# Moving the p_2 load behind the first expert tiles, and its transposes ahead of the gathered rows' transposes, in a two-block transformer kernel

## The chip, the cores and the metric

The kernel runs on one core of a Trainium2 chip. The metric is the device time of one execution in microseconds (us). Three runs of the kernel before took 2132.51, 2132.94 and 2133.28 us, median 2132.94. Everything is float32.

The engines are TensorE (PE, with its weight loads as PEld), VectorE (DVE), ScalarE (ACT), GpSimd (POOL) and SyncE (SP). SP does no arithmetic here; it waits on semaphores and issues nearly all DMA transfers.

## The reference

The input is one sequence of 256 tokens with 1024 features. A first block runs two layers, each a gated delta rule branch and a differential attention branch. A second block runs one layer: a pooling and dilated attention mixer, then a mixture of experts, then a gated projection of a second input `p` (256 tokens x 256 features), and a last norm. The change touches the passage from the mixer into the experts:

```python
x = x + jnp.einsum('bse,ed->bsd', mix, w_out[i])
x = x + moe(rmsnorm_2(x, g_ffn[i]), w_router[i], b_router[i], w_gate_up[i],
            b_gate_up[i], w_down[i], b_down[i])
gate = jax.nn.sigmoid(jnp.einsum('bsd,de->bse', rmsnorm_2(x, g_ple[i]), w_ple_gate[i]))
x = x + jnp.einsum('bsp,pd->bsd', p[i], w_ple_proj[i]) * gate
```

`moe` sends each token to its best 4 of 32 experts. An expert has a gate and up matrix of 1024 x 2048 and a down matrix of 1024 x 1024:

```python
gu = xb @ w_gate_up[e] + b_gate_up[e]
g, u = gu[:, :D_EXPERT], gu[:, D_EXPERT:]
g = jnp.minimum(g, SWIGLU_LIMIT)
u = jnp.clip(u, -SWIGLU_LIMIT, SWIGLU_LIMIT)
glu = g * jax.nn.sigmoid(SWIGLU_ALPHA * g)
return ((u + 1.0) * glu) @ w_down[e] + b_down[e]
```

## The kernel before

Each engine has its own program, written out by hand in order; there is no scheduler. An engine goes on in its order until a wait on a semaphore that another engine or a DMA raises. A transfer raises its semaphore by 16 when it has landed.

**The experts.** All 32 experts are computed for whatever tokens chose them, up to 64 tokens in one round. An expert's weights are six tiles of 2 MB: four of `w_gate_up_2` (j = 0 to 3) and two of `w_down_2` (j = 4, 5). The tiles T = 0, 1, 2, ... go round eight buffers of 2 MB in the order of `SEQ`; five of them are in the SBUF tensor `ring`, three in `region`. PE raises `tile_used` once for each tile that it is through with, and before the first expert by eight at once (L996). SP loads T0 to T3 while the mixer runs and T4 to T7 when the mixer has ended (`x_mixed` at 4), since their buffers hold mixer data until then. From T8 on SP waits for `tile_used` at T + 1, that is until PE is through with tile T - 8: T8 waits for T0, and T12 for T4, the first down tile of expert 0.

**SP around the change.** After `x_mixed`, SP issues in this order: `ptok` (the tokens of `p_2`, 256 KB, semaphore `ple_in`), the down biases (128 KB), the two gate and up biases (128 KB each) and `one_of` (80 KB) on `bias_in`, then T4 to T7, then the waiting loads from T8 on. All have line L402, that of the helper `load`. A row that names `p_dram` is the load of `ptok`.

**PE before the first expert.** The router's ranks end in one-hot matrices `P1` (DVE, L2100). `gather()` (L1006) multiplies them with `h2` and so picks the rows of expert 0 into bank 3. ACT copies them into `Xs` (L1487, semaphore `X_sb`), `turn_gathered()` transposes them on PE (L1013, `XT_ps`), and ACT copies the result into `XT` (L1491, `XT_sb`). Expert 0 begins when `XT_sb` is there: its bias products (L1054), then its gate and up products (L1062), the gather for expert 1, `down_biases()` (L1035), transposes (L1074, L1078, L1013) and the down products (L1088).

**The transposes of ptok** (L1100, four of 128 x 128 into bank 2, after a wait for `ple_in` at 16) stand between `turn_gathered()` and expert 0. ACT copies them into `pT` at L1497 (`pT_sb`), after its copy into `XT`. `pT` is used by `down_biases()` only as a wait (bank 2 must be free), and as data after the last expert.

Of the kernel before, what the change touches and what calls it, by code (L numbers as in the profile page):

```python
# [13 lines left out]
P = 128  # L14
# [105 lines left out]
def block_kernel(nc, a, out):  # L120
    ctx = ExitStack()
    with ctx:
# [5 lines left out]
        def s(name):  # L128

            if name not in sems:  # L130
                sems[name] = ctx.enter_context(nc.semaphore(name))
            return sems[name]
# [8 lines left out]
        def once(signal):  # L141
            return next(s(name) for name, signals in ONCE.items() if signal in signals)
# [89 lines left out]
        def view(at, n):  # L232
            return region[:, at:at + n]
# [16 lines left out]
        def units(ap):  # L250
            return ap.rearrange("p (u c) -> p u c", c=P)
# [43 lines left out]
        T, V = units(T_f), units(V_f)  # L295
# [26 lines left out]
        ptok = view(2048, 512).rearrange("p (t c) -> p t c", t=NT)  # L322
# [77 lines left out]
        def _(sp):  # L400
            def load(dst, src, name, **kw):
                sp.dma_start(dst, src, **kw).then_inc(s(name), 16)  # L402
# [56 lines left out]
            for n in range(4):  # L459
                c = (n + 1) % 4 * NB  # L460
# [20 lines left out]
            def expert_tile(T, e):  # L481

                j, slot = T % 6, SEQ[T % 8]
                if j < 4:
                    src = gate_up_src[ds(e * D + j * 256, 256), :].rearrange("(p k) n -> p (k n)", k=2)
                else:
                    src = down_src[ds(e * D + (j - 4) * 512, 512), :].rearrange("(p k) n -> p (k n)", k=4)
                load(slot_mem(slot), src, f"w_in_slot{slot}")
# [6 lines left out]
            load(brow, a["b_router_2"].broadcast_to([P, NE]), "ffn_in")  # L495
            load(grow, a["g_ffn_2"].broadcast_to([P, D]), "g_ffn_in")
            sp.wait_ge(s("x_mixed"), 4)
            load(ptok, a["p_2"][0, 0].rearrange("(t p) c -> p t c", p=P), "ple_in")
            load(biases[0:NE, :], a["b_down_2"][0], "bias_in")
            for g in range(2):  # L500
                load(biases[NE * (g + 1):NE * (g + 2), :], a["b_gate_up_2"][0, :, g * D:(g + 1) * D], "bias_in")
            load(one_of, a["c_one_of"], "bias_in")
            for T in range(4, 8):
                expert_tile(T, T // 6)
            for T in range(8, 6 * GROUP):
                sp.wait_ge(s("tile_used"), T + 1)
                expert_tile(T, T // 6)
# [16 lines left out]
            for u in range(4):  # L524
                t, g = divmod(u, 2)
# [6 lines left out]
        def _(pe):  # L532
# [38 lines left out]
            for l in range(DEPTH):  # L571
# [14 lines left out]
                for u in range(12):  # L586
# [4 lines left out]
                    for b in range(2):  # L591
                        c = (2 * (u % 2) + b) * P
# [50 lines left out]
                for u in range(12):  # L643
                    t = u % 2
# [199 lines left out]
                for u in range(4):  # L844
                    t, g = divmod(u, 2)
# [164 lines left out]
            def turn_gathered():  # L1010

                for c in range(4):
                    mm = pe.transpose(pb[3][:, c * P:(c + 1) * P], Xs4[:, c // 2, c % 2, :], ident)  # L1013
                mm.then_inc(s("XT_ps"), 1)
# [77 lines left out]
            pe.wait_ge(s("onehot"), 1)  # L1092
            pe.wait_ge(s("h2_sb"), NT)
            gather()
            pe.wait_ge(s("X_sb"), 1)
            turn_gathered()
            pe.wait_ge(s("ple_in"), 16)
            for t in range(NT):
                for k in range(2):
                    mm = pe.transpose(pb[2][:, k * S + t * P:k * S + (t + 1) * P], ptok[:, t, k * P:(k + 1) * P], ident)  # L1100
            mm.then_inc(once("pT_ps"), 1)
            for q in range(GROUP):
                expert(0, q)
            rounds = pe.value_load(rounds_i[0:1, 0:1], min_val=1, max_val=ROUNDS)
# [36 lines left out]
        def _(act):  # L1141
# [347 lines left out]
            def turned(n):  # L1489
                act.wait_ge(s("XT_ps"), n)  # L1490
                act.activation(XT, pb[3][:, :].rearrange("p (c h t) -> p c h t", c=4, h=2), ACT.Copy).then_inc(s("XT_sb"), 1)  # L1491

            act.preload_act_table_set("sigmoid_and_others")
            gathered(1)
            turned(1)
            await_once(act, "pT_ps")
            act.activation(pT, pb[2][:, :].rearrange("p (k t) -> p k t", k=2), ACT.Copy).then_inc(once("pT_sb"), 1)  # L1497

            def sigmoids(i):
                act.wait_ge(s("g_clamped"), i + 1)  # L1500
                act.activation(sg, gm, ACT.Sigmoid, scale=1.702).then_inc(s("sig"), 1)  # L1501
# [724 lines left out]
```

## Time and profile before

| | |
|---|---|
| median of 3 runs | 2132.94 us (2132.51 to 2133.28) |
| the profiled execution's own time | 2132.51 us |
| its span, first to last instruction | 2130.7 us |
| PE busy | 2040.8 us, 96% |
| DVE, ACT, POOL busy | 739.3, 445.9, 106.7 us |
| moved by DMA | 551.27 MB, mean 259 GB/s |
| mean granted TensorE clock | 0.990 of full speed |

The time is 1.8 us more than the span, and what lies outside the span is not touched here. Busy shares alone do not say what bounds the kernel: PE is busy for 96% of the span, in the expert stage too, yet a chain of waits can still pass through a transfer. The sections of the profile to read together are the rate of the DMA over the span, the chain that ended last, and the order of SP's transfers with the time at which each landed.

### The profile page before, as it was taken

Reading aid. Unit: us, or ns where it says so; the run is one execution under the profiler, and the core shown is the slowest. Engines: PE = TensorE matmul, PEld = TensorE weight load, DVE = VectorE, ACT = ScalarE, POOL = GpSimd, SP = SyncE. Lnnn points to the kernel's source line nnn. Section 1 sums busy time; section 2 is a strip of 40 time slices with the busy share of each in tenths; the row PEclk is TensorE's granted clock in tenths of the full one; section 3 lists DMA queues with packets and bytes.
Section 4 is the critical chain, followed back from the end, with each engine's and each line's share of the span. In section 5 each row is a group of like instructions: output and inputs, shape, how many; then the busy total and the mean of one; then the engine's idle time right before and its main releaser. Section 6 shows DMA issues by size and latency. Waiting matters only on the chain.

```text
span 2130.7 us, 23346 instructions
## 1 busy us (share of the span) xinstructions
PE 2040.8 (96%) x9042; PEld 1043.9 (49%) x9042; DVE 739.3 (35%) x2021; ACT 445.9 (21%) x1073; POOL 106.7 (5%) x84
## 2 busy tenths in 40 slices
PE   7999999999999999999998999999999999999998
PEld 6754777544875577644454333333333333333334
DVE  4559566211567665511143111111111111111112
ACT  2151454311124245311131000000000000000003
POOL 0022121000013112000000000000000000000000
PEclk9999999999999999999998999999999999999999
DMA  6643211342453312236634999999999999999993
GB/s 215 238 152 125 80 41 40 119 158 95 158 223 119 119 41 80 80 118 247 231 127 180 401 428 428 428 428 428 428 428 428 428 428 429 428 428 428 428 426 116
DMA packets 103066, 551.27 MB, mean 259 GB/s; under 512 B 9005, under 2 KB 13521, under 8 KB 77906
## 3 DMA queue, kind: packets, MB, share of 16 engines
q1 hardware_dynamic: 101138, 549.73, 64.1%
q8 instruction: 47, 0.77, 0.1%
q10 hardware_dynamic: 1856, 0.56, 0.1%
q14 instruction: 25, 0.20, 0.0%
HBM read 547.07 MB, written 3.21 MB: 258 GB/s over the span
## 4 chain that ended last, share of the span: by engine, by line
PE 77%; DMA 17%; DVE 4%; ACT 1%; issue 1%; SPq 0%; DVEq 0%; ACTq 0%
PE bank L557 26%; PE bank L1062 13%; DMA ring<-w_gate_up_dram 8%; DMA region<-w_gate_up_dram 8%; PE bank L1088 7%; PE bank L807 5%; PE bank L669 3%; PE bank L860 3%; PE bank L1020 2%; PE bank L1006 2%; PE bank L681 2%; PE bank L944 1%; PE bank L692 1%; PE bank L1054 1%; DVE region L1873 1%
## 5 line engine op out<-in xcount | busy, mean ns | idle before, releaser
L1062 PE MATMUL bank<-ring,region 128*64 128x512 f32 x1280 | 286.3, 596 | 16.2 <-DMA ring<-w_gate_up_dram 16.2
L2135 DVE TENSOR_SCALAR region<-bank 128x512 f32<-128x512 f32 x32 | 22.1, 692 | 718.1 <-PE bank L1062 718.1
L557 PE MATMUL bank<-ring,hT 128*128 128x512 f32 (+1 forms) x464 | 194.8, 577 | 0.0
L1062 PEld LDWEIGHTS bank<-ring,region 128*64 128x64 f32 x1280 | 87.6, 137 | 212.1 <-issue 174.3
L1062 PE MATMUL bank<-region 128*64 128x512 f32 x768 | 172.2, 595 | 13.5 <-DMA region<-w_gate_up_dram 13.5
L557 PE MATMUL bank<-ring,region 128*128 128x512 f32 x400 | 175.3, 598 | 4.5 <-ACT region L1154 4.5
L557 PE MATMUL bank<-hT,ring 128*128 128x256 f32 x768 | 173.8, 389 | 3.4 <-DMA ring<-w_in_dram 3.4
L557 PEld LDWEIGHTS bank<-hT,ring 128*128 128x128 f32 x768 | 149.2, 195 | 27.2 <-issue 6.0
L1088 PE MATMUL bank<-ring,region 128*64 128x512 f32 x640 | 142.6, 595 | 10.5 <-DVE region L2145 6.9
L557 PEld LDWEIGHTS bank<-ring,hT 128*128 128x128 f32 x464 | 87.5, 190 | 99.9 <-issue 98.5
L1501 ACT ACTIVATE region<-region 128x512 f32<-128x512 f32 x32 | 20.2, 630 | 519.8 <-DVE region L2135 519.8
L557 PEld LDWEIGHTS bank<-ring,region 128*128 128x128 f32 x400 | 76.0, 191 | 100.3 <-issue 95.0
L669 PE MATMUL bank<-ring,hT 128*128 128x512 f32 x256 | 123.2, 593 | 0.0
L1062 PEld LDWEIGHTS bank<-region 128*64 128x64 f32 x768 | 53.1, 137 | 129.8 <-issue 103.0
L807 PE MATMUL bank<-ring,hT 128*128 128x512 f32 x256 | 111.5, 592 | 0.0
L1088 PEld LDWEIGHTS bank<-ring,region 128*64 128x64 f32 x640 | 47.4, 137 | 89.2 <-issue 89.2
L1088 PE MATMUL bank<-region 128*64 128x512 f32 x384 | 86.2, 597 | 3.5 <-DVE region L2145 3.5
L2201 POOL TENSOR_TENSOR region<-ring,c_main_sb 128x512 f32<-128x512 f32 x48 | 64.4, 1346 | 281.9 <-PE bank L681 281.9
L1668 DVE SCALAR_TENSOR_TENSOR region<-region,conv_wT 128x256 f32<-128x256 f32 x192 | 78.0, 477 | 0.0
L807 PEld LDWEIGHTS bank<-ring,hT 128*128 128x128 f32 x256 | 48.0, 190 | 57.4 <-issue 57.4
L1505 ACT ACTIVATE region<-bank 128x512 f32<-128x512 f32 x32 | 19.1, 597 | 222.2 <-PE bank L1088 222.2
L1006 PE MATMUL bank<-region 128*64 128x512 f32 x264 | 63.7, 604 | 0.2 <-DVE region L2100 0.2
(343 smaller groups left out, 2350.3 us busy)
## 6 DMA issues: line engine op xcount, KB each, us to landing
ring<-w_gate_up_dram SPq DMA_DIRECT2D x80, 2048.0 KB, 31.0
region<-w_gate_up_dram SPq DMA_DIRECT2D x48, 2048.0 KB, 32.2
ring<-w_in_dram SPq DMA_DIRECT2D x44, 2048.0 KB, 7.9
ring<-w_down_dram SPq DMA_DIRECT2D x40, 2048.0 KB, 35.3
region<-w_down_dram SPq DMA_DIRECT2D x24, 2048.0 KB, 35.3
ring<-w_out_dram SPq DMA_DIRECT2D x5, 2048.0 KB, 7.9
ring<-rows_scratch SPq DMA_DIRECT2D x4, 2048.0 KB, 9.7
ring<-w_pa_dram SPq DMA_DIRECT2D x4, 2048.0 KB, 7.7
```

Source lines behind the costliest of these rows:

```text
L557: mm = pe.matmul(dst, lhs(k), w(k), start=(k == 0), stop=(k == n_k - 1))
L669: mm = pe.matmul(pb[3][:, :], hT[:, k, t * P:(t + 1) * P], w[:, k, :], start=(k == 0), stop=(k == KC - 1))
L681: mm = pe.matmul(pb[V_BANK[q]][:, u * P:(u + 1) * P], Lv[q][:, u, :], T[:, u, :], start=True, stop=True)
L807: mm = pe.matmul(pb[GATE_BANKS[kind][t]][:, :], hT[:, k, t * P:(t + 1) * P], w[:, k, :], start=(k == 0), stop=(k == KC - 1))
L860: mm = pe.matmul(pb[i % 4][:, :], hT[:, k, t * P:(t + 1) * P], slot_w(slot)[:, k, :], start=(k == 0), stop=(k == KC - 1))
L1006: mm = pe.matmul(pb[3][hf * 64:(hf + 1) * 64, :], P1[:, t, :], h2[:, t, hf * NB:(hf + 1) * NB], start=(t == 0), stop=(t == 1))
L1020: mm = pe.matmul(pb[4 + 2 * t + hf][:, :], CT[hf * 64:(hf + 1) * 64, t, :], ysb[hf * 64:(hf + 1) * 64, :], start=False, stop=False, skip_g ...
L1062: mm = pe.matmul(pb[g][hf * 64:(hf + 1) * 64, :], XT[:, 2 * (j % 2) + kk, j // 2, :], wj[:, kk, c:c + NB], start=False, stop=(j == 3 and k ...
L1088: mm = pe.matmul(pb[2][hf * 64:(hf + 1) * 64, :], actT[:, c, j, :], wj[:, c, hf * NB:(hf + 1) * NB], start=(j == 0 and c == 0), stop=(j == ...
L1668: ins = dve.scalar_tensor_tensor(dst, src, w, dst, ALU.mult, ALU.add)
L2135: dve.tensor_scalar(gm, pb[0][:, :], 7.0, None, ALU.min).then_inc(s("g_clamped"), 1)
L2201: pool.tensor_tensor(Lv[q].rearrange("p (d t) c -> p d t c", d=2), LT_all[:, n].rearrange("p (d t) c -> p d t c", d=2), lvl[:, q].unsqueez ...
```

## The change

It has three parts. On SP, T4 is issued first after `x_mixed`, then the biases and `one_of`, then T5 to T7, and `ptok` last, ahead of the first load that waits for `tile_used`. On PE, the wait for `ple_in` and the four transposes of `ptok` stand ahead of the wait for `X_sb` and `turn_gathered()`. On ACT, the copy into `pT` stands ahead of the copy into `XT`. Nothing is added or removed. Lines behind L498 move by one.

```diff
--- before.py
+++ after.py
@@ -495,13 +495,14 @@
             load(brow, a["b_router_2"].broadcast_to([P, NE]), "ffn_in")
             load(grow, a["g_ffn_2"].broadcast_to([P, D]), "g_ffn_in")
             sp.wait_ge(s("x_mixed"), 4)
-            load(ptok, a["p_2"][0, 0].rearrange("(t p) c -> p t c", p=P), "ple_in")
+            expert_tile(4, 0)
             load(biases[0:NE, :], a["b_down_2"][0], "bias_in")
             for g in range(2):
                 load(biases[NE * (g + 1):NE * (g + 2), :], a["b_gate_up_2"][0, :, g * D:(g + 1) * D], "bias_in")
             load(one_of, a["c_one_of"], "bias_in")
-            for T in range(4, 8):
+            for T in range(5, 8):
                 expert_tile(T, T // 6)
+            load(ptok, a["p_2"][0, 0].rearrange("(t p) c -> p t c", p=P), "ple_in")
             for T in range(8, 6 * GROUP):
                 sp.wait_ge(s("tile_used"), T + 1)
                 expert_tile(T, T // 6)
@@ -1092,13 +1093,13 @@
             pe.wait_ge(s("onehot"), 1)
             pe.wait_ge(s("h2_sb"), NT)
             gather()
-            pe.wait_ge(s("X_sb"), 1)
-            turn_gathered()
             pe.wait_ge(s("ple_in"), 16)
             for t in range(NT):
                 for k in range(2):
                     mm = pe.transpose(pb[2][:, k * S + t * P:k * S + (t + 1) * P], ptok[:, t, k * P:(k + 1) * P], ident)
             mm.then_inc(once("pT_ps"), 1)
+            pe.wait_ge(s("X_sb"), 1)
+            turn_gathered()
             for q in range(GROUP):
                 expert(0, q)
             rounds = pe.value_load(rounds_i[0:1, 0:1], min_val=1, max_val=ROUNDS)
@@ -1492,9 +1493,9 @@
 
             act.preload_act_table_set("sigmoid_and_others")
             gathered(1)
-            turned(1)
             await_once(act, "pT_ps")
             act.activation(pT, pb[2][:, :].rearrange("p (k t) -> p k t", k=2), ACT.Copy).then_inc(once("pT_sb"), 1)
+            turned(1)
 
             def sigmoids(i):
                 act.wait_ge(s("g_clamped"), i + 1)
```

SP's program from the wait for `x_mixed` to the first wait for `tile_used`, before. `p_dram` is the source of `ptok`; T4 and T5 come from `w_down_dram`, T6 and T7 from `w_gate_up_dram`, and the last row is T8 and T9.

```order
L402 DMA region<-p_dram 128x2x256 [waits x_mixed]
L402 DMA region<-b_down_dram 32x1024
L402 DMA region<-b_gate_up_dram 32x1024 x2
L402 DMA region<-c_one_of_dram 128x160
L402 DMA region<-w_down_dram 128x4096 x2
L402 DMA ring<-w_gate_up_dram 128x4096
L402 DMA region<-w_gate_up_dram 128x4096
L402 DMA ring<-w_gate_up_dram 128x4096 [waits tile_used] x2
```

The same place now:

```order
L402 DMA region<-w_down_dram 128x4096 [waits x_mixed]
L402 DMA region<-b_down_dram 32x1024
L402 DMA region<-b_gate_up_dram 32x1024 x2
L402 DMA region<-c_one_of_dram 128x160
L402 DMA region<-w_down_dram 128x4096
L402 DMA ring<-w_gate_up_dram 128x4096
L402 DMA region<-w_gate_up_dram 128x4096
L402 DMA region<-p_dram 128x2x256
L402 DMA ring<-w_gate_up_dram 128x4096 [waits tile_used] x2
```

The load of `ptok` has moved past the biases, `one_of` and all four tiles, and T4 has moved ahead of the biases.

PE's program from the gather to expert 0, before. L1006 is the gather, L1013 the transposes of the gathered rows, L1100 those of `ptok`, L1054 the first products of expert 0.

```order
L1006 MATMUL bank<-region 64x512 [waits h2_sb,onehot]
L1006 MATMUL bank<-region 64x512 x3
L1013 MATMUL bank<-c_main_sb,region 128x128 [waits X_sb]
L1013 MATMUL bank<-c_main_sb,region 128x128 x3
L1100 MATMUL bank<-c_main_sb,region 128x128 [waits ple_in]
L1100 MATMUL bank<-c_main_sb,region 128x128 x3
L1054 MATMUL bank<-region 64x512 [waits chosen,XT_sb]
```

And now, where L1007, L1099, L1014 and L1055 are the same four:

```order
L1007 MATMUL bank<-region 64x512 [waits h2_sb,onehot]
L1007 MATMUL bank<-region 64x512 x3
L1099 MATMUL bank<-c_main_sb,region 128x128 [waits ple_in]
L1099 MATMUL bank<-c_main_sb,region 128x128 x3
L1014 MATMUL bank<-c_main_sb,region 128x128 [waits X_sb]
L1014 MATMUL bank<-c_main_sb,region 128x128 x3
L1055 MATMUL bank<-region 64x512 [waits chosen,XT_sb]
```

The rows that wait for `ple_in` now stand ahead of those that wait for `X_sb`, and so ahead of everything in expert 0.

ACT's program at the same place, before. L1487 copies the gathered rows, L1491 their transposes, L1497 those of `ptok`.

```order
L1493 ACT_TABLE_LOAD
L1487 ACTIVATE region<-bank 128x512 [waits gather_ps]
L1491 ACTIVATE region<-bank 128x512 [waits XT_ps]
L1497 ACTIVATE region<-bank 128x512 [waits pe_once]
L1501 ACTIVATE region<-region 128x512 [waits g_clamped]
```

And now, where they are L1488, L1492 and L1497:

```order
L1494 ACT_TABLE_LOAD
L1488 ACTIVATE region<-bank 128x512 [waits gather_ps]
L1497 ACTIVATE region<-bank 128x512 [waits pe_once]
L1492 ACTIVATE region<-bank 128x512 [waits XT_ps]
L1502 ACTIVATE region<-region 128x512 [waits g_clamped]
```

The copy that waits for the transposes of `ptok` (`pe_once`) now stands ahead of the one that waits for `XT_ps`.

## Rows read from the trace of the kernel before

**Rows 1.** The page's second part: GB/s of all DMA in 40 slices.

```profile
GB/s 215 238 152 125 80 41 40 119 158 95 158 223 119 119 41 80 80 118 247 231 127 180 401 428 428 428 428 428 428 428 428 428 428 429 428 428 428 428 426 116
```

**Rows 2.** The chain that ended last, late in the expert stage: start, us, what.

```profile
2033.32 34.26 DMA region<-w_gate_up_dram
```

**Rows 3.** Windows: us; busy PE, PEld, DVE, ACT, POOL; clock; DMA share; GB/s.

```profile
1145.00:1146.00 1.00, 0.01 (x1) 0.00 (x0) 1.00 (x4) 1.00 (x4) 0.00 (x0) 1.00 0.89 233
...
1169.00:1170.00 1.00, 1.00 (x8) 0.39 (x6) 0.00 (x0) 0.00 (x0) 0.00 (x0) 1.00 0.00 0
...
1191.00:1192.00 1.00, 1.00 (x6) 0.31 (x4) 0.00 (x0) 0.00 (x0) 0.00 (x0) 1.00 0.04 16
1192.00:1193.00 1.00, 1.00 (x8) 0.40 (x6) 0.00 (x0) 0.00 (x0) 0.00 (x0) 1.00 0.00 0
...
1505.00:2067.00 562.00, 524.07 (x2488) 179.14 (x2482) 91.02 (x209) 46.00 (x76) 0.00 (x0) 1.00 1.01 428
```

**Rows 4.** SP's transfers in order of time: start us, us, queue, line, what.

```profile
1143.89 0.38 SPq L402 DMA_DIRECT2D region<-p_dram  x1
...
1146.21 0.91 SPq L402 DMA_DIRECT2D region<-w_down_dram  x2
...
1147.64 0.45 SPq L402 DMA_DIRECT2D region<-w_gate_up_dram  x1
1169.16 3.76 SPq L402 DMA_DIRECT2D ring<-w_gate_up_dram  x2
...
1192.27 3.76 SPq L402 DMA_DIRECT2D region<-w_gate_up_dram  x2
```

**Rows 5.** Transfers issued from 1143.5 to 1148: count, KB each, us to landing.

```profile
region<-w_gate_up_dram SPq DMA_DIRECT2D x1, 2048.0 KB, 22.4
region<-p_dram SPq DMA_DIRECT2D x1, 256.0 KB, 3.1
```

**Rows 6.** The same view of the transfer issued from 1169 to 1170.

```profile
ring<-w_gate_up_dram SPq DMA_DIRECT2D x1, 2048.0 KB, 7.7
```

**Rows 7.** The same view of the transfers issued from 1040 to 1100.

```profile
region<-c_count_dram SPq DMA_DIRECT2D x1, 256.0 KB, 13.0
```

**Rows 8.** The chain that ended last, from the gather into expert 0.

```profile
1159.01 3.34 PE bank L1006 x8
...
1162.37 0.60 ACT region L1487
...
1163.02 0.76 PE bank L1013 x4
...
1163.80 0.60 ACT region L1491
...
1164.45 1.09 PE bank L1054 x8
...
1179.42 1.74 PE bank L1006 x8
...
1186.40 0.85 PE bank L1078 x4
1187.26 0.85 PE bank L1013 x4
```

**Rows 9.** The timeline: start us, us, engine, line, what, count, idle before.

```profile
1159.16 0.24 DVE L2106 TENSOR_SCALAR region<-ones,region 128x64 f32<-128x64 f32 x1
...
1163.60 0.60 PE L1100 MATMUL bank<-c_main_sb,region 128*128 128x128 f32 x4
...
1164.30 0.59 ACT L1497 ACTIVATE region<-bank 128x512 f32<-128x512 f32 x1
```

**Rows 10.** Windows again, for the granted clock (third number from the end).

```profile
1148.00:1149.00 1.00, 1.00 (x8) 1.00 (x7) 0.37 (x1) 0.53 (x3) 0.00 (x0) 0.58 0.92 299
...
1161.00:1162.00 1.00, 1.00 (x4) 0.01 (x2) 0.28 (x2) 0.00 (x0) 0.00 (x0) 0.59 0.99 426
...
1186.00:1189.00 3.00, 3.00 (x13) 2.06 (x14) 1.95 (x6) 0.60 (x1) 0.00 (x0) 0.50 0.99 426
```

## The prediction

> **What bounds the kernel now.** I read the rate of the DMA over the span first. From the middle of the span on it stands at 428 GB/s and does not move until the last slice but one [rows 1]. That is a stream at its limit, and its length is fixed by its bytes. The late windows say the same: from 1505 to 2067 us the DMA moves 428 GB/s, while PE is busy for 524 of 562 us [rows 3], so PE has room and the DMA has none. The chain that ended last agrees: late in the expert stage its long pieces are waits for a weight tile, such as the one of 34.26 us that begins at 2033.32 [rows 2].
>
> A stream with no gaps can only end earlier if it starts earlier or carries less. So the next question is where its last gap lies. There are two windows with hardly a byte in them: 1169 to 1170 us, and 1191 to 1193 us [rows 3]. SP's issues explain both. T8 is issued at 1169.16, when PE is through with T0, and T12 at 1192.27, when PE is through with T4 of expert 0 [rows 4]. In both gaps the DMA has finished all it was given and waits for PE to free a buffer. Behind T12 it is never idle again. I checked that the rest is rigid: T12 to T189 (the last gate and up tile) are 178 tiles of 2.097 MB, which at 428 GB/s take 872.2 us; started at about 1193.0 they are through at 2065.2, and the last such wait in the chain ends at 2033.32 + 34.26 = 2067.58 [rows 2]. The difference of 2.4 us is what a landing adds.
>
> This gives the rule for the sum: the end of the kernel moves by as much as the issue of T12 moves, and T12 moves with the start of expert 0. Before expert 0 the order is gather at 1159.01, ACT copy at 1162.37, transposes at 1163.02, ACT copy at 1163.80, first product at 1164.45 [rows 8]. That short chain is what the change edits.
>
> **Part 1, T4 ahead of the small loads.** T4 is issued at 1143.89 instead of 1146.21, 2.32 us earlier [rows 4]. On its own this is worth nothing: T4 to T7 are read from about 1188 on (T4) and later, and the last of them has landed at 1147.64 + 22.4 = 1170.0 [rows 4, 5]. T8 still waits for PE, not for the queue. The loads on `bias_in` now land behind T4. T4 alone would take 7.7 us, as T8 did with an empty queue [rows 6], so to 1151.6, and the 464 KB of small loads behind it need 1.1 us at 428 GB/s and 2.0 us at the 233 GB/s of the window in which small loads ran [rows 3]: by 1154 they are there. Their first reader, the product with `one_of` on DVE, runs at 1159.16 [rows 9]. The cover is 5 us, so this costs 0.
>
> **Part 2, ptok behind T7.** Before, it landed 3.1 us after its issue, at 1147.0 [rows 5], far ahead of its transposes at 1163.60 [rows 9]. Now it is issued where T7 was or 0.5 us later, at about 1148, and four tiles stand ahead of it. The row of a load of exactly its size behind other data shows what that does: `c_count`, also 256 KB, took 13.0 us to land [rows 7]. And T7, issued at 1147.64 behind three tiles, took 22.4 [rows 5]. So I take the queue as first in, first out.
>
> When does it land? Lower bound: T4 lands 7.7 us after 1143.89, three more tiles follow at 2.097 MB / 428 GB/s = 4.9 us each, and all the small loads together (720 KB) take 1.7 us at the full rate: 1143.89 + 7.7 + 14.7 + 1.7 = 1168.0. Upper bound: nothing is won by the new order, T7 lands at 1170.0 as before and `ptok` 0.3 us behind it, 1170.3. Small loads ran at 233 GB/s rather than 428, which adds 1.4 us to the lower bound, but part of that lay in the start of the queue. I take 1168.9.
>
> **Part 3, the new wait.** On PE the transposes of `ptok` now stand ahead of the wait for `X_sb`. The gather ends at about 1162.35, and PE then stands still until 1168.9. Queued behind the waiting instruction are `turn_gathered()` and all of expert 0; ACT waits for both sets of transposes, DVE for the first products, and SP for `tile_used`. Nobody else has work that fills the time.
>
> While PE stands still for 6.5 us, its clock matters. In the trace the clock went to half at about 1148, after PE had done nothing from 1145 to 1146.5 and then only 32-column products [rows 3, 10], and it came back inside the window of 1161 to 1162, some 2.8 us after the gather had begun [rows 8, 10]. So I expect half clock (1.2 GHz) when PE starts again. What this is worth: the gather took 3.34 us with the clock mostly at half, and the same eight matmuls 1.74 at full [rows 8].
>
> The new chain: four transposes back to back at half clock take 0.85 us [rows 8]; the second set, with its end not overlapped, about 1.1 (0.76 at full clock, of which the pipelined part doubles) [rows 8]; then 0.04 to ACT, 0.60 for the copy into `XT`, and 0.05 back to PE, all as before [rows 8]. ACT's copy into `pT` of 0.59 us [rows 9] starts when the first set is done and is over before the second set is, so it is covered, by 0.5 us. Expert 0 starts at 1168.9 + 0.85 + 1.1 + 0.69 = 1171.54, where it was 1164.45: 7.1 us later. If the clock stays full, the two sets take 0.58 (start to start, 1163.02 to 1163.60) and 0.76 [rows 8, 9], and it is 6.5 us.
>
> Then the rest of the half clock. With the clock back 2.8 us after PE's start, at 1171.7, it costs nothing more. But the work in that time is thin (eight transposes and a pause for ACT), so I place the return later, near 1174: the bias products (1.09 us at full [rows 8]) cost 1.0 us more and the first gate products 0.2. The bounds of this term are 0 and 3.0.
>
> One thing I can't size: the clock was also at half from 1186 to 1189 [rows 10], inside expert 0, which costs half of 3 us, 1.5. In the shifted run it may fall out, or come at another place and cost as much again. I take 0 for the change, with 1.5 to either side.
>
> **What the edit doesn't win.** The transposes of `ptok` leave the place between `turn_gathered()` and expert 0. They ran from 1163.60 to 1164.20, while PE waited for the ACT copy that ended at about 1164.40 [rows 8, 9]. They were hidden; taking them away is 0.
>
> **Sum.** 7.1 + 1.2 = 8.3 us. Made against the profiled execution's own time of 2132.51 us it gives 2140.8. That execution was the fastest of the three, 0.43 under their median, so I forecast 2141.2. The bounds of the single terms together: at the low end 1168.0 with full clock (5.6) and the half clock in expert 0 gone (1.5), 4.1 us; at the high end 1170.3 (8.5), 3.0 and 1.5, 13.0 us.
>
> **Rivals.**
> - *No wait: ptok overtakes the tiles.* It is decided in the queue, between 1148 and 1162.35. If `ptok` lands before 1162.35, PE never waits: its transposes fill the 0.65 us in which `X_sb` is awaited, ACT does the `pT` copy while PE turns the rows, and expert 0 starts at 1164.45 give or take 0.3. Time 2132.5 to 2133.2, no change. For it: the 3.1 us that the load took with the queue empty. Against it: 13.0 and 22.4 us behind other data [rows 5, 7]. The Trainium skill, "DMA: Bandwidth & Descriptors", section "Queues, rings and completion order", says that completion is not in order per issuing engine: a later small transfer that uses fewer DMA engines can be complete while an earlier one is not. By that rule, if it bit here, the time would be that of this rival; the same section has each DMA engine consume its descriptors in ring order. No row here shows an overtaking. 9%.
> - *The wait is there but the clock holds.* Then the cost is 5.6 to 6.5 us plus nothing: 2138.5 to 2139.5. For it: in all of the DMA's own stretch from 1505 to 2067, with its 38 us of idle PE, the mean clock is 1.00 [rows 3]. Against it: the fall at 1148 after less idleness in one piece [rows 10]. 20%.
> - *The wait is there, but the stream takes it up.* PE starts later, yet T4 to T7 are already in place, so if the issue of T12 had slack the end wouldn't move in full; 2134 to 2137. For it: the mean PE need per expert is below that of the stream. Against it: both gaps in the stream [rows 3] are waits for PE, so there is no slack to spend. 6%.
> - *Faster.* The tiles in front free the stream 2.3 us earlier, and the wait is absent: 2130.2. It needs T8 to be bound by the queue, but it is issued at 1169.16 into a window in which hardly a byte moves [rows 3, 4]. 2%.
>
> The forecast itself, wait and slow clock, has 63%.
>
> **Chances.** A measurement of this kernel tells apart about 0.2%, 4.3 us. Slower by more than that is the forecast, the second rival, and a small part of the third: 0.86. Within: 0.12. Faster: 0.02. The range of 2137.3 to 2144.3 leaves out the first and last rival, most of the third, and the two far ends of the bounds.
>
> **What would show it.** In the profile of the changed kernel: `ptok` takes about 21 us to land; PE stands still from 1162.4 to about 1169 ahead of the four transposes of `ptok`, released by the DMA of `p_dram`; the granted clock in the windows from 1166 to 1172 is 0.5; the first L1055 product comes near 1171.5; T8 is issued near 1177.5 and T12 near 1200.6; the stream's gap ahead of T8 is some 10 us long instead of 1, and the one ahead of T12 about as long as it was; behind T12 all rows read as before, shifted. I am wrong if `ptok` lands within a few us (first rival), or if T12's issue moves by much less than expert 0's start (third).

## The result, and the profile after

Slower, as forecast, but by half as much again. The changed kernel takes 2145.72 us (median of 4 runs, 2144.22 to 2147.35) against 2132.76 (2132.51 to 2133.28). The ratio is 1.0058, 95% interval 1.0042 to 1.0075. I had forecast 2141.2, with a range up to 2144.3. The profiled execution took 2146.05 us, span 2144.2, so 13.5 us more than that of before.

The chain that ended last, from SP's issue of the `p_2` load (in `ptok`) into expert 0 (start us, us, what; lines are one higher than before, L1099 are the transposes of `ptok`):

```profile
1148.31 22.40 DMA region<-p_dram
1170.71 0.04 issue
1170.75 1.11 PE bank L1099 x4
1171.87 0.87 PE bank L1014 x4
1172.73 0.02 issue
1172.76 0.60 ACT region L1492
1173.36 0.04 issue
1173.40 1.98 PE bank L1055 x8
1175.39 15.78 PE bank L1063 x64
1191.16 1.75 PE bank L1007 x8
...
1193.83 4.85 PE bank L1036 x8
...
1201.01 8.07 PE bank L1089 x32
```

Where [rows 8] had the gather, one set of transposes and two copies, there is now a transfer, two sets of transposes and one copy. It lands at 1170.71, and expert 0 begins at 1173.40 instead of 1164.45. Further down four pieces are longer than they were: L1055 1.98 us instead of 1.09, L1063 15.78 instead of 13.88, the down biases (L1036) 4.85 instead of 3.69, and the down products (L1089) 8.07 instead of 7.56. The same pieces in the chain of before, where the lines are one lower:

```profile
1165.54 13.88 PE bank L1062 x64
...
1182.09 3.69 PE bank L1035 x8
...
1188.11 7.56 PE bank L1088 x32
```

The timeline of PE at the start (start us, us, engine, line, what, and in brackets the idle time before it and what ended it) says who was waited for:

```profile
1159.36 3.28 PE L1007 MATMUL bank<-region 128*64 128x512 f32 x8 [0.22 <-DVE region L2101]
1170.75 1.11 PE L1099 MATMUL bank<-c_main_sb,region 128*128 128x128 f32 x4 [8.12 <-DMA region<-p_dram]
```

SP's issues, to be set beside [rows 4]:

```profile
1144.21 0.33 SPq L402 DMA_DIRECT2D region<-w_down_dram  x1
...
1147.78 0.48 SPq L402 DMA_DIRECT2D region<-w_gate_up_dram  x1
1148.31 0.45 SPq L402 DMA_DIRECT2D region<-p_dram  x1
1180.91 3.76 SPq L402 DMA_DIRECT2D ring<-w_gate_up_dram  x2
...
1205.68 3.76 SPq L402 DMA_DIRECT2D region<-w_gate_up_dram  x2
```

T12 is issued at 1205.68, 13.41 us later than before (0.32 of it because the mixer ended later), and the end has moved by 13.5. The time to landing of the same transfers, to be set beside [rows 5]:

```profile
region<-w_gate_up_dram SPq DMA_DIRECT2D x1, 2048.0 KB, 22.3
...
region<-p_dram SPq DMA_DIRECT2D x1, 256.0 KB, 22.4
```

T7 lands at 1147.78 + 22.3 = 1170.1 and `ptok` 0.6 us behind it. The windows (us; busy PE, PEld, DVE, ACT, POOL; granted clock; DMA share; GB/s), beside [rows 3, 10]:

```profile
1151.00:1155.00 4.00, 1.29 (x7) 1.16 (x6) 2.84 (x16) 1.63 (x3) 0.00 (x0) 0.50 1.06 272
...
1165.00:1166.00 1.00, 0.00 (x0) 0.00 (x0) 0.00 (x0) 0.00 (x0) 0.00 (x0) 0.76 1.00 426
1166.00:1170.00 4.00, 0.00 (x0) 0.00 (x0) 0.00 (x0) 0.00 (x0) 0.00 (x0) 0.50 0.77 313
1171.00:1179.00 8.00, 7.31 (x26) 2.84 (x27) 0.00 (x0) 1.19 (x2) 0.00 (x0) 0.50 0.00 0
...
1179.00:1180.00 1.00, 1.00 (x6) 0.31 (x6) 0.00 (x0) 0.00 (x0) 0.00 (x0) 0.92 0.00 0
1197.00:1203.00 6.00, 6.00 (x18) 2.97 (x19) 1.96 (x6) 0.60 (x1) 0.00 (x0) 0.50 0.86 366
1204.00:1206.00 2.00, 2.00 (x12) 0.73 (x10) 0.00 (x0) 0.00 (x0) 0.00 (x0) 1.00 0.00 0
1520.00:2080.00 560.00, 522.47 (x2480) 178.85 (x2476) 91.06 (x209) 46.00 (x76) 0.00 (x0) 1.00 1.01 428
```

The clock falls to half inside the wait, near 1165.5, and stays there until just after 1179, though PE is busy for 7.31 of the 8 us from 1171 on. From 1171 to 1179 the DMA moves nothing: this is the gap ahead of T8, which was 1 to 2 us. It lasts until T8 is issued at 1180.91, so some 10 us, as forecast. Late in the expert stage everything is as before.

**A yardstick for the experiments.** The mixer ends at another time in each execution (SP's first issue behind `x_mixed` lies between 1141.1 and 1144.9 us in these profiles), and that moves whole times by 3 us or more. So I read two lengths in each profile: from that first issue to the issue of T12, and from there to the end of the span. The first holds everything that the change touches. Both are lengths of one execution per kernel, and the granted clock differs between executions of the same kernel: in the last set of runs the kernel before took 2141.16 us at a mean clock of 0.985 and 2129.03 us at 0.992. A difference of 1 to 2 us in one profile can be that and nothing else.

Each ratio is taken against runs of the kernel before on the same chip; their medians were 2132.81, 2132.58 and 2132.99 us in the three sets of four, single runs from 2125.5 to 2141.2. The ratio is estimated from the single runs and is not the quotient of the medians.

| kernel | median us | ratio to before, 95% | first issue to T12 | T12 to the end |
|---|---|---|---|---|
| before | 2132.76 | | 48.38 | 938.4 |
| changed | 2145.72 | 1.0058 [1.0042, 1.0075] | 61.47 | 938.5 |
| sp_only | 2141.43 | 1.0041 [1.0024, 1.0058] | 58.94 | 938.4 |
| pe_act_only | 2132.04 | 0.9999 [0.9985, 1.0012] | 49.72 | 938.5 |
| ptok_after_one_tile | 2131.81 | 0.9989 [0.9975, 1.0004] | 48.31 | 938.4 |
| filled_wait | 2147.99 | 1.0072 [1.0050, 1.0095] | 65.16 | 938.6 |
| filled_wait_short | 2140.20 | 1.0035 [1.0024, 1.0047] | 55.96 | 938.4 |
| ptok_before_last_tile | 2138.40 | 1.0032 [1.0020, 1.0045] | 55.66 | 938.6 |
| late_transposes | 2138.94 | 1.0030 [1.0019, 1.0042] | 54.61 | 938.6 |
| ptok_on_act_queue | 2142.64 | 1.0034 [1.0020, 1.0049] | 58.43 | 938.6 |
| small_loads_first | 2144.87 | 1.0046 [1.0032, 1.0060] | 61.27 | 938.6 |
| late_transposes_filled | 2135.38 | 1.0014 [1.0000, 1.0028] | 55.52 | 938.7 |
| down_biases_in_expert_1 | 2130.83 | 0.9993 [0.9981, 1.0004] | 43.54 | 944.4 |
| down_biases_in_expert_3 | 2128.34 | 0.9979 [0.9965, 0.9993] | 43.27 | 940.8 |

Ten of the twelve experiments, with and without waits, end 938.4 to 938.7 us behind the issue of T12, as do before and changed. The rule that the end moves with T12 holds, as long as T12 goes into an empty queue and no new gap opens behind it. In the last two kernels T12 is issued while the queue still has work, so part of what it wins is not won at the end.

### The profile page after: what moved, and what is told of

It is laid out like the page before. It is cut to its first block, busy times and chain, and to the rows that moved or that the text cites. A ratio compares the mean times of both kernels' runs of the same rounds, so it can differ in the third digit from the quotient of the medians.

```text
span 2144.2 us, 23346 instructions
## 1 busy us (share of the span) xinstructions
PE 2046.5 (95%) x9042; PEld 1045.9 (49%) x9042; DVE 739.5 (34%) x2021; ACT 446.0 (21%) x1073; POOL 106.6 (5%) x84
## 4 chain that ended last, share of the span: by engine, by line
PE 76%; DMA 18%; DVE 4%; ACT 1%; issue 1%; SPq 0%; DVEq 0%; ACTq 0%
PE bank L558 26%; PE bank L1063 13%; DMA ring<-w_gate_up_dram 8%; DMA region<-w_gate_up_dram 8%; PE bank L1089 7%; PE bank L808 5%; PE bank L670 3%; PE bank L861 3%; PE bank L1021 2%; PE bank L1007 2%; PE bank L682 2%; PE bank L945 1%; PE bank L693 1%; PE bank L1055 1%; DMA region<-p_dram 1%; DVE region L1874 1%
## 5 line engine op out<-in xcount | busy, mean ns | idle before, releaser
L1063 PE MATMUL bank<-ring,region 128*64 128x512 f32 x1280 | 288.2, 599 | 16.2 <-DMA ring<-w_gate_up_dram 16.2
L2136 DVE TENSOR_SCALAR region<-bank 128x512 f32<-128x512 f32 x32 | 22.1, 692 | 730.1 <-PE bank L1063 730.1
L1063 PEld LDWEIGHTS bank<-ring,region 128*64 128x64 f32 x1280 | 88.0, 137 | 214.5 <-issue 176.5
L1063 PE MATMUL bank<-region 128*64 128x512 f32 x768 | 172.2, 595 | 13.6 <-DMA region<-w_gate_up_dram 13.6
L1089 PE MATMUL bank<-ring,region 128*64 128x512 f32 x640 | 142.6, 595 | 10.4 <-DVE region L2146 6.9
L1063 PEld LDWEIGHTS bank<-region 128*64 128x64 f32 x768 | 53.1, 137 | 129.8 <-issue 102.7
L1089 PEld LDWEIGHTS bank<-ring,region 128*64 128x64 f32 x640 | 47.4, 137 | 89.1 <-issue 89.1
L1089 PE MATMUL bank<-region 128*64 128x512 f32 x384 | 86.8, 600 | 3.5 <-DVE region L2146 3.5
L1007 PE MATMUL bank<-region 128*64 128x512 f32 x264 | 63.6, 604 | 0.2 <-DVE region L2101 0.2
```

Of the source, the lines that this page charges most:

```text
L1007: mm = pe.matmul(pb[3][hf * 64:(hf + 1) * 64, :], P1[:, t, :], h2[:, t, hf * NB:(hf + 1) * NB], start=(t == 0), stop=(t == 1))
L1063: mm = pe.matmul(pb[g][hf * 64:(hf + 1) * 64, :], XT[:, 2 * (j % 2) + kk, j // 2, :], wj[:, kk, c:c + NB], start=False, stop=(j == 3 and k ...
L1089: mm = pe.matmul(pb[2][hf * 64:(hf + 1) * 64, :], actT[:, c, j, :], wj[:, c, hf * NB:(hf + 1) * NB], start=(j == 0 and c == 0), stop=(j == ...
L2136: dve.tensor_scalar(gm, pb[0][:, :], 7.0, None, ALU.min).then_inc(s("g_clamped"), 1)
```

## The experiments

The theory: `ptok` stands at the end of SP's queue behind four tiles and PE waits for it (theory A), and PE, once it has stood still, works at half clock (theory C). The rivals are that the new order on PE and ACT makes the loss (B), that the late load slows the weight stream itself (D), and, for the last steps, that the DMA engines serve whatever comes first (E) and that the transposes of `ptok` had kept the clock up (F).

**sp_only.** PE and ACT as in the kernel before, SP as in the changed one. The edit on PE, against the changed kernel (ACT's two copies are put back in the same way):

```diff
             gather()
+            pe.wait_ge(s("X_sb"), 1)
+            turn_gathered()
             pe.wait_ge(s("ple_in"), 16)
...
-            pe.wait_ge(s("X_sb"), 1)
-            turn_gathered()
```

> The changed kernel with the orders of PE and ACT put back; only SP's order of loads stays changed. Theory A (the place of the p_2 load in the DMA queue makes the loss): PE turns the gathered rows at once and then waits for the load, which again lands near 1170.7 us; only one set of transposes (about 1.1 us at half clock) stands between the landing and expert 0, and ACT's copy into XT is long done, so expert 0 starts near 1171.9 instead of 1173.4, and the time is 1 to 2 us under the changed kernel: 2143.5 to 2145. Theory B (the new order on PE and ACT makes most of the loss): 2133 to 2136.

Measured 2141.43, 2 us under the range of theory A and far from that of B. From the chain that ended last:

```profile
1145.46 21.48 DMA region<-p_dram
...
1166.99 1.11 PE bank L1101 x4
1168.10 1.92 PE bank L1055 x8
```

The wait is there, and first issue to T12 is 58.94 us instead of 61.47. Of these 2.5 us, 1.5 are the chain from the landing to expert 0 (1.16 us instead of 2.69, without the second set of transposes and the copy behind it). The other 0.9 is the landing itself, 25.6 us after the first issue here and 26.5 in the changed kernel, which the order on PE and ACT does not explain. So the order of SP's loads makes nearly all of the loss, and the order on PE and ACT adds 1.5 us to a wait that is there.

**pe_act_only.** The kernel before with the new order on PE and ACT (the edit above the other way round).

> The kernel before with only the orders of PE and ACT changed; SP's loads stay as before. Theory A: the load has landed at 1147, there is no wait, expert 0 starts at 1164.4 or 0.3 us later, time 2132.5 to 2133.3, the same as before. Theory B: 2136 or more.

Measured 2132.04, ratio 0.9999 (0.9985 to 1.0012). The transposes of `ptok` run in the time in which `X_sb` is awaited. From the end of the gather to expert 0 it is 2.47 us instead of 2.10, since the clock was still at half there, and in the time of the kernel nothing is lost or won. Its 49.72 us are 1.3 over before because its down biases met the half clock for longer (5.36 us instead of 3.69). B is out.

**ptok_after_one_tile.**

```diff
             load(one_of, a["c_one_of"], "bias_in")
+            load(ptok, a["p_2"][0, 0].rearrange("(t p) c -> p t c", p=P), "ple_in")
             for T in range(5, 8):
                 expert_tile(T, T // 6)
-            load(ptok, a["p_2"][0, 0].rearrange("(t p) c -> p t c", p=P), "ple_in")
```

> The changed kernel with the p_2 load issued after one_of, so behind one tile (T4) instead of four. Theory A: it lands at about 1154, before the gather ends at 1162.5, no wait is left, and T4 in front wins nothing: 2132.5 to 2133.3. Theory B: as the changed kernel, 2143 to 2147. A rival on the gain (the tiles in front start the stream of weights earlier): 2130 to 2131.5.

Measured 2131.81, ratio 0.9989 (0.9975 to 1.0004), 48.31 us to T12. Its time to landing:

```profile
region<-p_dram SPq DMA_DIRECT2D x1, 256.0 KB, 8.2
```

It landed at 1155.2, before the gather had ended at 1162.7, and the whole loss is gone. T4 in front wins nothing that can be seen either: 48.31 us against 48.38.

**ptok_before_last_tile.** The same line between T6 and T7.

> The changed kernel with the p_2 load issued ahead of T7, so behind three tiles instead of four. Theory A: it lands one tile (4.9 us) earlier, 17.5 us after its issue, near 1165.5; PE stands still for 3 us instead of 8. If the clock then holds, from the first issue behind x_mixed to T12 some 51 to 53 us, time 2135.5 to 2137.5; if it falls all the same, 54 to 56.5 us and 2138 to 2141. If the loss weren't set by the place in the queue: 61 us and 2144 to 2147.

Measured 2138.40; first issue to T12 55.66, inside the second of the cases given. It landed 17.9 us after its issue instead of 22.4; counted from the first issue that is 21.5 us instead of 26.5. PE stood still for 3.05 us, and the work behind that was at half clock all the same (1.98 us for the bias products, 15.08 for the gate and up products). The loss follows the place in the queue: 13.1 us to T12 behind four tiles, 7.3 behind three, nothing behind one.

**filled_wait.** 18 matmuls on PE in the place of the wait:

```diff
             gather()
+            for _ in range(18):
+                pe.matmul(pb[2][:, :], ident, h2[:, 0, 0:NB], start=True, stop=True)
             pe.wait_ge(s("ple_in"), 16)
```

> The changed kernel with 18 more matmuls (identity times h2, 128 x 512, results overwritten unread) on PE between the gather and the wait for ple_in; at full clock they take about 7.7 us and end near 1170.4, just before the load lands. Theory C (4.4 us of the loss are half clock, which follows from PE standing still): the clock stays full until the down biases, expert 0 starts 0.6 us earlier, its first products cost 2.8 us less, so 3.0 to 4.5 us under the changed kernel, 2141 to 2143, though PE does more work; what is left over before is the wait of 8.4 us alone. Rival (the half clock isn't due to the wait but to the kind of work in expert 0): the same as the changed kernel or slower by up to 1 us.

Measured 2147.99. I had sized the fill wrongly: each of these products is two instructions of 0.44 us, so they took 16.0 us and were themselves what expert 0 waited for. But behind them L1055 took 1.09 us and L1063 13.88, the figures of before.

**filled_wait_short.** The same with 9.

> As filled_wait, with 9 extra products instead of 18. The first try was twice too long: each product is two instructions of 0.44 us, so 18 took 16.0 us; 9 take about 8 us and end when the p_2 load lands. Theory C (standing still costs the clock): clock full in the first products of expert 0 (L1055 in 1.1 us, L1063 in 13.9 instead of 15.8), and from the first issue behind x_mixed to the issue of T12 57 to 59 us instead of 61.5; time 2139.5 to 2143. Rival (the half clock has another cause): 61 us or more, 2144 to 2147.

Measured 2140.20. The chain that ended last:

```profile
1162.94 8.26 PE bank L1097 x18
1171.20 0.62 PE bank L1101 x4
...
1172.98 1.09 PE bank L1055 x8
1174.07 13.88 PE bank L1063 x64
...
1190.62 3.70 PE bank L1036 x8
```

L1097 is the fill, L1101 the transposes of `ptok`. The load landed at 1148.87 + 22.2 = 1171.1, 26.2 us after the first issue, nearly as late as in the changed kernel (26.5). Yet the work behind it runs at full clock, and T12 comes 55.96 us after the first issue instead of 61.47, 1 us better than the range of theory C. This splits the loss of 13.1 us: expert 0 still starts 7.6 us later than before, which is the late load, and 5.5 us are gone. Of the 5.5, 0.3 is the earlier landing, 0.8 the chain from there to expert 0, 2.8 the first products, and 1.6 the down biases and down products. Only the first products and the chain ahead of them, 3.6 us, can be laid to the standstill: in filled_wait, which has no standstill either, the down biases and down products took 4.31 and 8.62 us, as much together as in the changed kernel (4.85 and 8.07).

Over all fourteen profiles, the first products of expert 0 ran at half clock in all five in which PE had stood still for 3 us or more, and at full clock in seven of the nine others; the two exceptions come next. So 8 us of work whose result nobody reads made the stretch shorter. In the whole times the gain over the changed kernel is just at the edge of what the runs tell apart (1.0024 to 1.0047 against 1.0042 to 1.0075).

**late_transposes.** SP as changed, but the transposes of `ptok` stand in `down_biases`, and ACT's copy behind its second copy of gathered rows. The added lines (the same ones are gone from in front of `turn_gathered()`):

```diff
+                pe.wait_ge(s("ple_in"), 16)
+                for t in range(NT):
+                    for k in range(2):
+                        mm = pe.transpose(pb[2][:, k * S + t * P:k * S + (t + 1) * P], ptok[:, t, k * P:(k + 1) * P], ident)
+                mm.then_inc(once("pT_ps"), 1)
                 await_once(pe, "gates_sb")
                 await_once(pe, "pT_sb")
```

> SP's order as in the changed kernel (the p_2 load last), but its transposes on PE stand in down_biases, after the products of expert 0's first four tiles, and ACT's copy behind the second gather. Theory A: the load lands 8 us before PE comes to it, no wait is left, and the time is that of the kernel before or 0.5 us over it for the transposes, which now stand on PE's path (0.4 to 0.9 us): 2132 to 2134; from the first issue behind x_mixed to T12 48.5 to 49.5 us. Theory D (the load at the end of the queue slows the stream itself, whatever PE does): 2140 or more.

Measured 2138.94, a miss: 6 us over what A said, with no wait. The chain that ended last:

```profile
1159.46 3.44 PE bank L1007 x8
...
1165.01 1.16 PE bank L1060 x8
1166.17 15.46 PE bank L1068 x64
1181.62 1.72 PE bank L1007 x8
1183.34 0.59 PE bank L1030 x4
...
1184.66 0.39 PE bank L1036 x2
...
1185.50 6.36 PE bank L1041 x8
```

and two windows:

```profile
1166.00:1169.00 3.00, 3.00 (x12) 1.00 (x10) 0.00 (x0) 0.00 (x0) 0.00 (x0) 0.50 0.87 351
...
1187.00:1196.00 9.00, 9.00 (x22) 4.00 (x22) 1.96 (x6) 0.60 (x1) 0.00 (x0) 0.50 0.63 269
```

Expert 0 starts at 1165.01, 20.6 us after the first issue, just as before, so A holds as far as the wait goes. But the first products take 1.6 us more at half clock; the transposes and a copy by ACT that `down_biases` awaits add 1.2 to the path; and the down biases and the first down tile cost 3.4 more, again at half clock. (In the windows between, the clock was full from 1163 to 1165, with PE busy for 0.42 and 0.32 us of these two, and fell near 1165.9, inside the bias products.) D is out: the stream itself behind T12 is as before. That the clock can cost this much without any wait for a load is what I had not allowed for.

**late_transposes_filled.** Four transposes of `h2` where those of `ptok` had stood:

```diff
             turn_gathered()
+            for c in range(4):
+                pe.transpose(pb[2][:, c * P:(c + 1) * P], h2[:, 0, c * P:(c + 1) * P], ident)
```

> late_transposes with four dummy transposes (of h2, results unread) where those of ptok stood before, in PE's pause for ACT's copy. late_transposes had no wait, yet lost 6.2 us between the first issue and T12: 1.6 at half clock in the first products, 1.2 for the copy of pT on PE's path, 3.4 at half clock in the down biases and down products. Theory F (the transposes of ptok in the pause were what kept the clock up): with the fill the first products take 13.9 us again, and T12 comes 49.5 to 52.5 us after the first issue (54.6 without), time 2133.5 to 2136.5. Rival (the clock falls by chance of phase): as late_transposes, 2137 to 2139.5.

Measured 2135.38 as the median, 3.6 us under late_transposes and inside the range of theory F. But the intervals of the two ratios overlap (1.0000 to 1.0028 and 1.0019 to 1.0042), and single runs lay between 2132.36 and 2144.07. The profiled execution, at 2137.83 us, does not bear F out: its clock stayed at half through the gather and the fill up to 3.7 us into the first products (L1068 15.72 us), and its 55.52 us are no better. So F is not shown, and what keeps the clock up at this place stays open.

**ptok_on_act_queue.** The load is taken from SP and issued by ACT ahead of its table load:

```diff
+            act.dma_start(ptok, a["p_2"][0, 0].rearrange("(t p) c -> p t c", p=P)).then_inc(s("ple_in"), 16)
             act.preload_act_table_set("sigmoid_and_others")
```

> The changed kernel with the p_2 load taken from the end of SP's queue and issued by ACT, behind the router's exponentials at about 1153.5, while the four tiles are still in flight. If the loss comes from the order within SP's one queue (theory A), a load on another queue is served beside the tiles: it lands in 3 to 6 us, by 1160, no wait is left, first issue to T12 48.2 to 50, time 2131 to 2133.5. If the DMA engines are simply busy and serve whatever comes first (rival E), it lands with T7 near 1170 and the time is 2143 to 2147.

Measured 2142.64, 0.4 us under the range of E and far over that of A. The landing lies between the two:

```profile
region<-w_gate_up_dram SPq DMA_DIRECT2D x1, 2048.0 KB, 22.7
...
region<-p_dram ACTq DMA_DIRECT2D x1, 256.0 KB, 14.6
```

It was issued at 1149.96 and landed at 1164.6, 3 us before T7 (1144.95 + 22.7 = 1167.7). So the second queue is served beside the first, and the load does overtake, but slowly: 14.6 us instead of 3.1. The Trainium skill, "DMA: Bandwidth & Descriptors", section "Queues, rings and completion order", has each DMA engine take turns between queues packet by packet. The overtaking agrees with that. An estimate of the size needs an assumption of mine, that a turn is one row; that section lets a packet hold several descriptors, so it does not give it. `ptok` has rows of 1 KB, 256 in all, 16 for each of 16 engines, and a tile has rows of 16 KB; an engine's share of 428 GB/s is 26.75, so a 16 KB row takes 0.61 us and 16 turns 9.8 us. With the 3.1 us of an empty queue that is 12.9, near the 14.6 measured. No run here tests the assumption.

**small_loads_first.** T4 is put back behind the small loads; only `ptok` is out of place.

```diff
             sp.wait_ge(s("x_mixed"), 4)
-            expert_tile(4, 0)
...
-            for T in range(5, 8):
+            for T in range(4, 8):
```

> The changed kernel with T4 back behind the small loads (down, gate and up biases, one_of), so only the p_2 load is out of place. It sizes the term of the landing: the forecast counted 1.1 us won by T4 in front and the changed kernel won nothing (T7 landed at 1170.1 in both). If T4 in front is worth nothing, T7 and the p_2 load land as long after the first issue as in the changed kernel, 26.5 us give or take 0.5, time 2144 to 2147. If it is worth something that another loss covered, 27.5 us or later, 2146 to 2148.

Measured 2144.87; `ptok` landed at 1148.09 + 22.1 = 1170.2, and T12 came after 61.27 us, nearly as in the changed kernel. The landing is 25.9 us after the first issue, 0.1 below the band that I gave, and within the 25.6 to 26.5 us of the kernels that have T4 in front and `ptok` last. T4 in front is worth nothing even for the queue's end. The window of 1151 to 1155 above fits this: behind T4 the small loads bring the queue down to 272 GB/s, a loss of 4 x (1 - 272 / 428) = 1.5 us, about what I had counted as won. In front they run while the queue starts up, at 188 to 262 GB/s from 1145 to 1149, and from 1144 to 1156 this kernel moves 328 GB/s and the changed one 300.

**down_biases_in_expert_1 and down_biases_in_expert_3.** These start from the kernel before and turn its own reading round: if a gap ahead of T12 is a wait for PE, what stands on PE ahead of T4's use can move. The biases' products go into a later expert; in the second one the first combine opens the sums, and the biases' products are added to them. The edit on PE in the second one (ACT's copy of the transposed gates moves along with it):

```diff
                 if first:
-                    down_biases()
+                    await_once(pe, "pT_sb")
                 else:
                     pe.wait_ge(s("y_sb"), i)
-                    combine()
+                    if isinstance(r, int) and i == 1:
+                        pe.wait_ge(s("rounds_known"), 1)
+                    if isinstance(r, int) and i == 3:
+                        down_biases()
+                    combine(isinstance(r, int) and i == 1)
```

> The kernel before (its order of loads and transposes) with down_biases moved from expert 0 to expert 1, ahead of its combine. If the gap in the weight stream ahead of T12 is a wait for PE, as read from before, T12 can be issued 3.7 to 5.2 us earlier, but the stream has data until about 1190.5, so 1.9 to 3 us of gap go and the time is 2129.5 to 2131. The 5 us then lie in expert 1, where the queue holds some 5 us of tiles ahead. Rival (that queue is too short, the gap comes back ahead of T18): 2132.5 to 2133.5.

Measured 2130.83, ratio 0.9993 (0.9981 to 1.0004), which is not told apart from no change. T12 came 4.8 us sooner, but the rival's mechanism is what the profile shows: the DMA stood still ahead of T18, issued at 1220.19, and the end lies 944.4 us behind T12, so the whole stretch is 1.1 us longer than before.

```profile
1219.00:1220.00 1.00, 1.00 (x7) 0.38 (x5) 0.00 (x0) 0.00 (x0) 0.00 (x0) 1.00 0.00 0
1220.00:1221.00 1.00, 1.00 (x8) 0.48 (x6) 0.00 (x0) 0.00 (x0) 0.00 (x0) 1.00 0.00 0
```

> The kernel before with down_biases moved to expert 3; expert 1's combine opens the sums instead. With it in expert 1, T12 was issued 4.8 us earlier, but a gap of 2.6 us came up ahead of T18 (end minus issue of T12 944.4 instead of 938.4). PE gains 2 us per expert on the stream, so by expert 3 the queue holds 4 us more and covers the 5.5 us of the down biases: no gap ahead of T12 nor later, 2 to 3 us less than before, 2129.5 to 2131. Rival: the gap only moves on to T30, 2132 to 2133.5.

Measured 2128.34, ratio 0.9979 (0.9965 to 0.9993): faster than both kernels, by some 0.2% against before, and more than I expected. Its windows around the place of the old gap and around expert 3:

```profile
1184.00:1185.00 1.00, 1.00 (x7) 0.35 (x4) 0.00 (x0) 0.00 (x0) 0.00 (x0) 1.00 1.15 492
1185.00:1186.00 1.00, 1.00 (x7) 0.37 (x5) 0.00 (x0) 0.00 (x0) 0.00 (x0) 1.00 0.73 311
1186.00:1187.00 1.00, 1.00 (x8) 0.49 (x6) 0.00 (x0) 0.00 (x0) 0.00 (x0) 1.00 1.15 492
...
1260.00:1300.00 40.00, 38.65 (x164) 14.74 (x166) 7.53 (x19) 3.47 (x7) 0.00 (x0) 0.91 1.00 421
```

No gap is left ahead of T12, where [rows 3] has two windows with hardly any data, and from 1187 to 1260 the rate is 427 to 428 GB/s. (A window of 1 us can read above the stream's rate, as 492 here; the three together give 431.) The half clock that went with the down biases now falls into expert 3 (mean clock 0.91 from 1260 to 1300), where the stream goes on at 421 GB/s. From the first issue to the end of the span it takes 984.1 us instead of 986.8, and these 2.7 us are what I expected; the rest of the gain in the median is beyond what one profile explains.

## Why the prediction was right in its mechanism and wrong in its size

- **What bounds the kernel** (the end moves with T12): right. The table shows 938.4 to 938.7 us from T12 to the end in every kernel but the last two.
- **Part 1, T4 in front is worth nothing, and the biases land in time**: right. `one_of` took 9.2 us and landed at 1155.4, later than the 1154 of my sum, but its reader runs four microseconds after that.
- **Part 2, the queue is first in, first out, `ptok` lands near 1168.9**: the order was right (the rival that it overtakes is out: no overtaking within SP's queue in any run), the size 1.8 us short. It landed at 1170.71, 0.4 beyond my upper bound; 0.3 of this is that the mixer ended later. I had counted on time won by T4's earlier issue; small_loads_first shows that there is none.
- **Part 3, the chain from the landing to expert 0**: 1.95 + 0.69 = 2.64 us forecast, 2.69 measured.
- **The half clock in the first products**: this is the step that failed. I took 1.2 us with a bound of 3.0; it is 0.9 + 1.9 = 2.8. I had read the return of the clock from the gather as 2.8 us after PE's start, and moved it to 5 us after the landing by judgement. That reading left out that PE had been at work on the router's small products since 1156.48, 5.3 us ahead of the return. In the changed kernel the clock came back 8.4 us after PE's start: through the transposes, the pause for ACT and the 32-row products of L1055 it was at half, and it returned 3.8 us into L1063. In late_transposes_filled it came 14.5 us after the first of the router's products.
- **The half clock in the down biases**, which I took as 0 with 1.5 to either side, cost 1.7: the down biases 1.16, the first down tile 0.5. This term failed with the one before it: together they were 1.2 us in the sum and 4.5 measured. It came out like this in kernels without a wait too (5.36 us for the down biases in pe_act_only, 6.36 in late_transposes), so I can't say that the change causes it. It also makes the gap ahead of T12 longer, which I had expected to stay as it was: the stream is down to 33 GB/s from 1202 on, and T12 is issued at 1205.68.
- **The sum**: 7.1 + 1.2 + 0 = 8.3 forecast; 8.95 (expert 0's start) + 2.8 + 1.7 = 13.4 measured. Of the 5.1 us missing, 1.9 are the later start (nearly all of it the landing) and 3.3 the clock. All three errors went the same way, and the range, drawn narrower than the terms' own bounds (up to 13.0 us), could not hold them.
- **The rival "the clock holds"** is out for the changed kernel, but filled_wait_short is that case built by hand: 7.6 us, where I had written 5.6 to 6.5.
- **The rival "the stream takes it up"** is out for the changed kernel: T12 moved by 13.4 us and the end by 13.5.

What stays open: which work keeps the clock up between the gather and expert 0, since late_transposes_filled gave a better median and a profile no better, and whether the 1.7 us in the down biases and down products belong to the change at all.

## What to carry to other kernels

A small load that something waits for goes ahead of the bulk in its queue, or several bulk transfers of time are added to it; another queue helps only in part. When a wait on TensorE is priced, the work behind it has to be priced at half clock as well, and for longer than the first few instructions: here the wait cost 7.6 us, the half clock tied to it 3.6, and another 1.7 at half clock came further down. And where a saturated stream sets the end, list the gaps in it and ask of each which instruction frees the next buffer; what stands ahead of that instruction is worth moving, to a place where the queue is deep enough.

## What the runs showed of the hardware

- The granted clock stayed at 1.2 GHz for some 8 us in which TensorE was busy 7.31 of 8 us (windows above) with transposes, 32-row products and at last 128-row ones. In the wait before that it had fallen from full to half 2.9 us after PE's last product.
- 8.3 us of unread matmuls in a wait went with a stretch that was 5.5 us shorter (55.96 against 61.47), of which 0.3 us was an earlier landing.
- A 256 KB load with rows of 1 KB took 3.1 us with the queues empty, 14.6 on a queue of its own beside tiles with rows of 16 KB, and 22.4 behind four of them.
